# Third norm from undivided rows, and a reordered end of the convolution tiles

## The reference, cut to what matters

```python
h_res = h_res + (silu(gu[..., :D_FF]) * gu[..., D_FF:]) @ w_down   # "down"
x = rmsnorm(h_res, final_norm_w)                                   # end of block 1
h = rmsnorm_2(x, norm_even)                                        # the third norm is both of these
a_val, a_glu, a_gate, b_val, b_gate = split(h @ w_in_even)
u = a_val * sigmoid(a_glu)                                         # "glu": eight pairs of units
u = causal_depthwise_conv(u, conv_w, conv_b)                       # 31 taps
```

## Time and profile before

| What | us |
|---|---|
| median of three runs | 1782.23 (1780.98 to 1783.13) |
| the profiled execution | 1781.74 |
| its span, first to last instruction | 1779.70 |
| PE busy | 1726.0 (97%) |
| DVE busy | 830.3 (47%) |
| ACT busy | 679.4 (38%) |
| POOL busy | 862.9 (48%) |

### The profile page before, as it was taken

One profiled execution on the slowest core, in us unless ns is written; L12 is line 12 of the kernel. 1 busy time (PEld: TensorE's weight loads), 2 busy tenths in 40 slices (PEclk: granted clock), 3 DMA queues, 4 the chain that ended last, 5 costly groups with the idle time before them and its releaser, 6 DMA issues.

```text
span 1779.7 us, 22744 instructions
## 1 busy us (share of the span) xinstructions
PE 1726.0 (97%) x9103; PEld 1453.8 (82%) x9103; DVE 830.3 (47%) x1329; ACT 679.4 (38%) x997; POOL 862.9 (48%) x482
## 2 busy tenths in 40 slices
PE   7999899999999999999999999999999999999997
PEld 7888789889988888877888887877887778888886
DVE  7678955724333201112111112116999963357753
ACT  5656443232232222234222223223233444356651
POOL 3456443232334544544555555445459566356661
PEclk9999989999999999999999999998999999999999
DMA  5475377444322224222222223331222322222332
GB/s 198 140 233 167 88 227 231 117 150 148 114 66 84 94 92 141 91 92 95 95 94 94 93 92 101 96 106 62 94 94 94 108 86 92 95 96 95 96 100 76
DMA packets 120720, 201.39 MB, mean 113 GB/s; under 512 B 32512, under 2 KB 71576, under 8 KB 120616
## 3 DMA queue, kind: packets, MB, share of 16 engines
q1 hardware_dynamic: 119128, 197.47, 35.1%
q10 hardware_dynamic: 1488, 2.48, 0.4%
HBM read 170.46 MB, written 29.46 MB: 112 GB/s over the span
## 4 chain that ended last, share of the span: by engine, by line
PE 87%; DVE 7%; ACT 2%; issue 1%; DMA 1%; SPq 1%; POOL 0%; DVEq 0%; ACTq 0%; POOLq 0%
PE ps L403 72%; PE ps L1741 4%; DVE cacc L2170 2%; PE ps L877 1%; DVE inv L617 1%; DMA d_p<-dec 1%; DVE prd L614 1%; PE ps L930 1%; PE ps L923 1%; PE ps L909 1%; PE ps L887 1%; PE ps L917 1%; PE ps L934 1%; PE ps L895 1%; PE ps L885 1%
## 5 line engine op out<-in xcount | busy, mean ns | idle before, releaser
L391 POOL TENSOR_TENSOR w_lo<-w_raw,w_hi 128x1024 fp32r<-128x1024 f32 x264 | 634.4, 2411 | 537.1 <-ACT w_hi L385 536.9
L403 PE MATMUL ps<-hp_hi,w_hi 128*128 128x512 f32 (+2 forms) x1664 | 557.5, 363 | 2.1 <-DVE cacc L2170 1.5
L403 PE MATMUL ps<-hp_lo,w_hi 128*128 128x512 f32 (+2 forms) x1664 | 552.6, 360 | 0.0
L403 PE MATMUL ps<-hp_hi,w_lo 128*128 128x512 f32 (+2 forms) x1664 | 552.4, 359 | 0.0
L403 PEld LDWEIGHTS ps<-hp_hi,w_hi 128*128 128x128 f32 x1664 | 297.0, 190 | 57.2 <-issue 6.1
L403 PEld LDWEIGHTS ps<-hp_lo,w_hi 128*128 128x128 f32 x1664 | 296.8, 190 | 50.6 <-issue 1.7
L385 ACT ACTIVATE w_hi<-w_raw 128x1024 fp32r<-128x1024 f32 x264 | 277.6, 1054 | 157.0 <-DMA w_raw<-in_w 148.2
L403 PEld LDWEIGHTS ps<-hp_hi,w_lo 128*128 128x128 f32 x1664 | 296.6, 190 | 48.2
L1223 DVE SCALAR_TENSOR_TENSOR ps<-u_in,par,ps 128x511 f32<-128x511 f32 (+14 forms) x240 | 176.6, 739 | 8.4 <-ACT ps L1215 0.9
L2170 DVE SCALAR_TENSOR_TENSOR cacc<-ps,par,cacc 128x528 f32<-128x528 f32 x96 | 73.6, 766 | 34.5 <-ACT cacc L1789 31.8
L2552 POOL TENSOR_TENSOR y_lo<-tmp,y_hi 128x512 fp32r<-128x512 f32 x22 | 28.4, 1292 | 105.5 <-ACT y_hi L1953 105.5
(11 more groups left out here) (403 smaller groups left out, 2542.6 us busy)
## 6 DMA issues: line engine op xcount, KB each, us to landing
w_raw<-in_w SPq DMA_DIRECT2D x264, 512.0 KB, 3.5
d_y<-zero SPq DMA_DIRECT2D x6, 688.0 KB, 6.1
d_x<-zero SPq DMA_DIRECT2D x6, 688.0 KB, 5.9
d_at<-at SPq DMA_DIRECT2D x16, 256.0 KB, 2.9
d_kc<-kc SPq DMA_DIRECT2D x16, 256.0 KB, 3.1
d_qd<-eg SPq DMA_DIRECT2D x16, 256.0 KB, 3.1
d_p<-dec SPq DMA_DIRECT2D x16, 256.0 KB, 3.2
AT<-d_at SPq DMA_DIRECT2D x16, 256.0 KB, 5.7
```

The costliest lines, as they stand in the source:

```text
L391: e.tensor_tensor(w_lo[:, u % RAW, :], w_raw[:, u % RAW, :], w_hi[:, u % RAW, :].bitcast(F32), ALU.subtract).then_inc(s_lo, 1)
L403: mm = e.matmul(ov, w, r[:, k, t0:t1], start=(first and n == 0 and p3 == 0), stop=(last and n == len(tiles) - 1 and p3 == 2))
```

## The change

**The end of the tiles.** For tiles 15 to 22 ACT rounds the unit of tile n+2 behind `act_tap(n)` and no longer at the start of its iteration. In iteration 23 ACT first does `act_tap(23)`, the rounding, `act_vtm(2)` and `act_msb(0)`, and only then the silu of tile 22. `act_pg(4)` moves from behind the tiles to iteration 24, in front of `act_vt(3)`; `pe_pk(4)` moves from between `pe_msa(1)` and `pe_yx(0, 0)` to between `pe_vt(3)` and `pe_vtm(3)`.

**The third norm.** While `down` runs, ACT rounds x times the two weights, undivided, to h_hi, and DVE subtracts h_lo. PE begins `glu` with these; the column sums stand behind its first unit and the spread behind its second. The products of the first three pairs are multiplied in PSUM by the token's factor, row(7), on DVE (`pair_scaled`). Beside that DVE divides the eight rows into yb, ACT rounds n_hi, POOL subtracts n_lo, and pairs 3 to 7 and all later units up to `bgate` multiply these. The convolution steps are dealt out as 4, 10, 10 and five times 13 in `glu`, and 35 in place of 20 behind `bval`. Several buffers change their address; in the second mixer n_hi and n_lo take the place of h_hi and h_lo.

```diff
+GLU_STEPS = [4, 10, 10, 13, 13, 13, 13, 13]
 BV_STEPS = [4, 4, 3, 15, 7, 10, 14, 28]
 BG_STEPS = [6, 6, 6, 6, 5, 2, 0, 0]
...
-        24: [("pgp", 4), ("vt", 3), ("vtm", 3)]}
+        24: [("pgp", 4), ("pgq", 4), ("vt", 3), ("pkp", 4), ("vtm", 3)]}
...
+        h0 = top[0]
         hp_hi = put("hp_hi", [P, KT, T1 + 4], F32R)
         hp_lo = put("hp_lo", [P, KT, T1 + 4], F32R)
...
-        mx_lo = z("mx_lo", [P, 2 * KT, SEQ], 3 * K16, F32R)
+        mx_lo = at("mx_lo", [P, 2 * KT, SEQ], h0, F32R)
         u_in = z("u_in", [P, KT, SEQ], K16)
-        sg_a = z("sg_a", [P, KT, SEQ], 3 * K16)
+        sg_a = at("sg_a", [P, KT, SEQ], h0)
+        n_hi = z("n_hi", [P, KT, SEQ], 3 * K16, F32R)
+        n_lo = z("n_lo", [P, KT, SEQ], 4 * K16, F32R)
         yb = z("yb", [P, KT, SEQ], 5 * K16)
         pv = z("pv", [P, KT, 16 + SEQ], 5 * K16)
...
@@ -1517,7 +1521,6 @@
 
             pe_t(e, 0, 0, 32)
             pe_msa(e, 1)
-            pe_pk(e, 4)
             pe_yx(e, 0, 0)
             pe_msb(e, 1)
...
-            e.wait_ge(*ad.at("down", 2 * KT - 2))
-            pe_cols(e, row(7), 0).then_inc(ss.sem, 1)
-            pe_cols(e, row(4), 4).then_inc(ss.sem, 1)
-            e.wait_ge(*rc.at("n3", 5))
-            pe_spread(e, 5, 32).then_inc(tb_.sem, 1)
-
-            e.wait_ge(*dv.at("down", KT))
...
             u = BASE["glu"]
-            e.wait_ge(s_lo, u + 2)
-            for lo_part in (False, True):
-                for k in range(KT):
...
+            for j in range(KT):
+                rows, width = ((h_hi, h_lo), TOK) if j < 3 else ((n_hi, n_lo), ALL)
+                ready = {0: lambda k: hh.at("n3u", k + 1), 3: lambda k: lo.at("n3", k + 1)}.get(j)
+                e.wait_ge(*(dv.at("glu", j - 1) if j >= 2 else dv.at("down", 2 * j + 5)))
+                gemm(e, u + 2 * j, [ps[:, 2 * (j % 2), :]], width, *rows, K8, ready=ready).then_inc(s_pe, 1)
+                if j == 0:
+                    e.wait_ge(*ad.at("down", 2 * KT - 2))
+                    pe_cols(e, row(7), 0).then_inc(ss.sem, 1)
+                    pe_cols(e, row(4), 4).then_inc(ss.sem, 1)
+                e.wait_ge(*(ev.at("glu", j - 1) if j >= 2 else dv.at("down", 2 * j + 6)))
+                gemm(e, u + 2 * j + 1, [ps[:, 2 * (j % 2) + 1, :]], width, *rows, K8).then_inc(s_pe, 1)
+                if j == 0:
+                    e.wait_ge(*rc.at("n3", 5))
+                    pe_spread(e, 5, 32).then_inc(tb_.sem, 1)
 
             for j in range(KT):
                 e.wait_ge(*(ev.at("bval", j - 3) if j >= 4 else ev.at("glu", 7 + j // 2) if j % 2 else dv.at("glu", 7 + j // 2)))
-                gemm(e, BASE["bval"] + j, [ps[:, j % 4, :]], TOK, h_hi, h_lo, K8).then_inc(s_pe, 1)
+                gemm(e, BASE["bval"] + j, [ps[:, j % 4, :]], ALL, n_hi, n_lo, K8).then_inc(s_pe, 1)
...
-                if n < len(TILES):
+                if n < 15:
                     round_unit(e, n + 2)
+                if n == 23:
+                    act_tap(n)
+                    round_unit(e, n + 2)
+                    act_vtm(e, 2)
+                    act_msb(e, 0)
...
-                    if n != 3:
+                    if n not in (3, 23):
                         act_tap(n)
+                    if 15 <= n < 23:
+                        round_unit(e, n + 2)
...
-                    if task == "vtm":
+                    if task == "vtm" and n != 23:
...
-                    if task == "msb":
-                        act_msb(e, arg)
-                    if task == "pg":
+                    if task in ("pg", "pgq"):
                         act_pg(e, arg)
...
-            act_pg(e, 4)
             act_tc(e, 0, 0, 32)
...
+                if j == 0:
+                    e.wait_ge(*dg.at("g2", 1))
+                e.activation(h_hi[:, j, META:T1], x[:, j, :], ACT.Copy, scale=small[:, 36 + j:37 + j]).then_inc(hi.sem, 1)
...
+            round_unit(e, BASE["glu"] + 2)
+            round_unit(e, BASE["glu"] + 3)
             e.wait_ge(*ss.at("n3", 2))
             e.activation(small[:, 16:20], ps[:, 4, 4:8], ACT.Sqrt, bias=eps_col).then_inc(rt.sem, 1)
             e.wait_ge(*rc.at("n3", 3))
             e.activation(small[:, 28:32], small[:, 24:28], ACT.Sqrt, bias=eps_col).then_inc(rt.sem, 1)
-            for k in range(KT):
+            round_unit(e, BASE["glu"] + 4)
+            e.wait_ge(*tb_.at("n3", 1))
+            e.activation(row(7), ps[:, 5, :], ACT.Copy).then_inc(rt.sem, 1)
+
+            def divided_hi(k):
                 e.wait_ge(*hh.at("n3", k + 1))
-                e.activation(h_hi[:, k, META:T1], row(k), ACT.Copy).then_inc(hi.sem, 1)
+                e.activation(n_hi[:, k, :], yb[:, k, :], ACT.Copy).then_inc(hi.sem, 1)
+
...
-                round_unit(e, BASE["glu"] + 2 * j + 2)
-                round_unit(e, BASE["glu"] + 2 * j + 3)
-                e.wait_ge(s_pe, BASE["glu"] + 2 * j + 2)
+                if j >= 2:
+                    round_unit(e, BASE["glu"] + 2 * j + 2)
+                    round_unit(e, BASE["glu"] + 2 * j + 3)
+                e.wait_ge(*(fd.at("n3", 2 * j + 1) if j < 3 else (s_pe, BASE["glu"] + 2 * j + 2)))
                 if j >= 2:
...
-                if j in (3, 5):
-                    act_uc(e, (j - 3) // 2)
-                    act_c0(e, (j + 1) // 2)
+                if j == 0:
+                    for k in range(KT):
+                        divided_hi(k)
+                        if k == 3:
+                            round_unit(e, BASE["glu"] + 5)
+                if j in (4, 7):
+                    act_uc(e, (j - 4) // 3)
+                    act_c0(e, 2 + (j - 4) // 3)
 
...
+                if j >= 1:
+                    e.wait_ge(*hi.at("n3u", j))
+                    e.scalar_tensor_tensor(h_lo[:, j - 1, META:T1], x[:, j - 1, :], small[:, 35 + j:36 + j], h_hi[:, j - 1, META:T1].bitcast(F32),
+                                           ALU.mult, ALU.subtract).then_inc(hh.sem, 1)
...
-            e.wait_ge(*dg.at("g2", 1))
-            e.wait_ge(*tb_.at("n3", 1))
-            for k in range(KT):
-                e.scalar_tensor_tensor(row(k), x[:, k, :], small[:, 36 + k:37 + k], ps[:, 5, :], ALU.mult, ALU.mult).then_inc(hh.sem, 1)
-
+
+            def pair_scaled(j, part):
+                b = 2 * (j % 2) + part
+                e.wait_ge(s_pe, BASE["glu"] + 2 * j + 1 + part)
+                e.tensor_tensor(ps[:, b, :], ps[:, b, :], row(7), ALU.mult).then_inc(fd.sem, 1)
+
+            def divided(k):
+                e.scalar_tensor_tensor(yb[:, k, :], x[:, k, :], small[:, 36 + k:37 + k], ps[:, 5, :], ALU.mult, ALU.mult).then_inc(hh.sem, 1)
+
+            e.wait_ge(*rt.at("n3", 3))
             n0 = 0
             for j in range(KT):
+                if j < 3:
+                    pair_scaled(j, 1)
+                    if j == 0:
+                        divided(0)
+                    pair_scaled(j, 0)
+                    e.wait_ge(*fd.at("n3", 2 * j + 2))
                 e.wait_ge(*ev.at("glu", j + 1))
                 e.tensor_tensor(u_in[:, j, :], row(j % 2), ps[:, 2 * (j % 2), :], ALU.mult).then_inc(dv.sem, 1)
-                conv_steps(e, n0, 13)
-                n0 += 13
+                if j == 0:
+                    for k in range(1, KT):
+                        divided(k)
+                conv_steps(e, n0, GLU_STEPS[j])
+                n0 += GLU_STEPS[j]
 
             e.wait_ge(*dv.at("glu", KT))
             for r in range(4):
@@ -2386,8 +2415,8 @@
                 n += 1
                 conv_steps(e, n0, BV_STEPS[j])
                 n0 += BV_STEPS[j]
-            conv_steps(e, n0, 20)
-            n0 += 20
+            conv_steps(e, n0, 35)
...
-            for k in range(KT):
+            def divided_lo(k):
                 e.wait_ge(*hi.at("n3", k + 1))
-                e.tensor_tensor(h_lo[:, k, META:T1], row(k), h_hi[:, k, META:T1].bitcast(F32), ALU.subtract).then_inc(lo.sem, 1)
+                e.tensor_tensor(n_lo[:, k, :], yb[:, k, :], n_hi[:, k, :].bitcast(F32), ALU.subtract).then_inc(lo.sem, 1)
+
             for j in range(2 * KT):
                 split_unit(e, BASE["glu"] + j + 2)
+                if j in (2, 3):
+                    for k in range(4 * (j - 2), 4 * (j - 2) + 4):
+                        divided_lo(k)
```

More of the change, by code:

```diff
@@ L1675, in pe_program @@
                 e.wait_ge(*(dv.at("bgate", j - 3) if j >= 4 else ev.at("pool", j + 5)))
-                gemm(e, BASE["bgate"] + j, [ps[:, j % 4, :]], TOK, h_hi, h_lo, K8).then_inc(s_pe, 1)
+                gemm(e, BASE["bgate"] + j, [ps[:, j % 4, :]], ALL, n_hi, n_lo, K8).then_inc(s_pe, 1)
                 if j in (0, 4, 7):
@@ L1706, in pe_program @@
                         e.wait_ge(*l_sg.at(3 * g - 2 + i))
-                    gemm(e, BASE[f"xr{g}"] + i, [ps[:, xr_bank(g, i), :]], TOK, h_hi, h_lo, K8,
+                    gemm(e, BASE[f"xr{g}"] + i, [ps[:, xr_bank(g, i), :]], ALL, n_hi, n_lo, K8,
                          ready=(lambda k: hh.at("n4", k + 1)) if g == 0 and i == 0 else None).then_inc(s_pe, 1)
```

(6 more changed lines are left out.)

48 lines of the change are left out of this document (16 added, 32 removed).

## The result

The changed kernel takes 1771.09 us, the median of six runs (1767.55 to 1774.78), where the kernel before, beside it, takes 1783.15: a ratio of 0.9931, 95% interval 0.9917 to 0.9945. That is 12.1 us faster; forecast were 13.0, and 1769.0 with a range of 1762.0 to 1775.5. The profiled execution took 1772.52 with a span of 1770.7 (before 1779.7), so the two profiles show only 9 of the 12 us. The lines of the code have moved on: L407 is the product of a weight unit (L403 before), L395 POOL's split (L391), L1227 a step of the convolution (L1223), L1231 act_uc (L1227).

The account below looks back on a forecast made before the run. PE, busy 97% of the span, bounds the kernel, so edits pay only where it waits. Tail 5.8 plus third norm 7.2 (11.79 - 1.1 - 3.45) gives 13.0 us: 1769.0, range 1766.0 to 1771.5 (wider 1762.0 to 1775.5).

Parts of the forecast that it names:

- Third norm on PE: From the end of `down` to `glu`'s first pair: 25.46 us becomes 13.67, gain 11.79, part of it clock.
- The blocked add: Third norm: POOL's split holds up DVE's last `row(7)` add, so PE waits 1.1 us before the column sums (0 to 2.4).
- DVE up to `glu`: After the third norm's spread: the convolution starts 8 us later, about 1219, and nothing is late in `glu`.
- The debt of 15 steps: Convolution steps moved behind `bval`: ACT waits for DVE, PE waits 2.85 before `pool` 2 and 0.6 more; cost 3.45 us (0 to 8).
- Two covers: Behind `bval`: lateness of act_uc(4) in `agate` hidden by 0.6 us, that of `bgate` 4's wait hidden by 0.35.
- (a): QKV tail: moving pe_pk(4) off the chain between pe_msa(1) and pe_yx gains 3.72 us (1.9 to 5.4).
- (b): QKV tail: act_tap(23) no longer queues behind tile 22's silu, DVE's 1.30 us wait goes; counted only as cover for (a).
- (c): Tiles 15 to 22: rounding behind act_tap keeps splits off the substitution, which ends 2.1 us earlier (-2.4 to +4.3).
- The tail: End of the QKV tiles and first slots: 3.72 from (a) plus 2.1 from (c), 5.8 us gained and carried through the slots.
- The sum: Whole kernel: 5.8 plus 7.2 us is 13.0 faster; profiled 1781.74 becomes 1768.7, stated as 1769.0.
- the clock falls in the wait at `pool`: Rival: PE's clock drops in the new 2.85 us wait at `pool`, price 3.7 us, giving 1772.4; chance 0.10.
- The locks undo (a) and (c): Rival, QKV tail: DVE and POOL blocking each other leaves the tail's gain at 0, giving 1774.5; chance 0.08.

Follow-up runs that it names:

- deal: Changed kernel with convolution steps dealt out otherwise (more in `glu`, `bgate`'s first product ahead of steps) and ACT's copies 4 and 5 later; 1768.89 us.
- uc45_late: Changed kernel with act_uc(5), act_c0(7) moved behind `pool` 1's evictions and act_uc(4), act_c0(6) to `agate` 4; end of `down` to span's end 580.3 us for 576.8.
- r17_back: Changed kernel with only unit 17's rounding (tile 15's turn) back in front of the silu; ratio 0.9914 to the kernel before.
- r17_pk_back: r17_back with pe_pk(4) and its exponentials also back between pe_msa(1) and pe_yx; ratio 0.9938 to the kernel before.
- round_back: Changed kernel with the roundings of tiles 15 to 22 back in front of the silu and the tap; ratio 0.9950 to the kernel before.
- the second trace: The changed kernel as it is, profiled and timed again beside later variants; median 1768.18 us.

## Why the prediction was right, step by step

- **Third norm on PE, 11.79.** Measured 25.46 - 13.87 = 11.59. Right, its part through the clock too (13.7 us at 1.2 GHz around the old norm, none around the new one).
- **The blocked add, 1.1.** Did not occur: PE has no gap there in any of the twelve traces of the new third norm. The split starts at 1197.51 as placed, but DVE's instructions stand back to back there, and POOL's took 3.04 instead of 2.40: the split was held up, not the add.
- **DVE up to `glu`.** The convolution starts at 1215.61, 7.87 behind the spread (8 forecast), and nothing was late in `glu`: DVE stood idle for 1.38 and 2.11 before pairs 2 and 3.
- **The debt of 15 steps, 3.45.** The wait at `pool` was 3.11 for 2.85, with the cause as named (deal and uc45_late show it). Two covers were thinner than I said. act_uc(4), hidden by 0.6, cost 0.7: not through the rounding, but through sg_a, whose eviction stands behind it. In all the stretch grew by 236.5 - 231.4 = 5.1. Of that 3.1 and 0.7 are the waits named, 0.4 one that the trace puts down to issue. Most of the other 0.9 lies at the same three places: a matmul's row is 0.16 longer than the 0.233 from start to start, so each idle time is 0.16 short, and the first matmul behind it takes some 0.1 more (1389.55 to 1389.88, and not 0.233). The term is mis-sized by 1.6, the add of 1.1 did not occur: 11.59 - 5.1 = 6.5 against 7.2 (E-D: 6.6).
- **(a) pe_pk(4), 3.72.** 4.8 in the comparison of r17_back and r17_pk_back, one trace each, inside its bounds (1.9 to 5.4) and near the upper one, for the reason given there: L881 and L824 get the clock back.
- **(b)** The wait of 1.30 before the taps of tile 23 is gone and the taps of 22 and 23 run back to back (214.31 to 220.55). It was more than cover: by round_back, its rounding of unit 25 behind the tap frees one step and ends the substitution 2.2 earlier. The prediction saw this block go, but took it for replaced by one of unit 24 and gave (b) nothing.
- **(c) The roundings, 2.1.** This step failed. One blocked step of 2.42 is left of four, the one forecast for unit 24; the block forecast at tile 17 did not come. Tile 15's taps came late as forecast (1.47 for 1.7). Yet the substitution ends only 0.8 earlier, measured from A (54.5 for 55.2), and by round_back the moved roundings of (c) alone make it 1.4 later. What I did not follow was PE: I let DVE be even again by tile 19 and took the tiles for DVE's. Tile 17 waits for those taps, and after a gap of 2.95 runs in part at 1.2 GHz. It costs 3.0 and PE's tiles end 0.5 later than before, not earlier. Of the 0.7 that the scatter still gained, the weight load took the rest. X came no earlier, so (b) and (c) together were worth 0. With unit 17 left alone they are worth 2.7 (B-A 63.37), with the load moved 3.6.
- **The tail, 5.8.** 5.05 in the second trace (C-A), 0.2 in the first, where slot 0 at the low clock took 4.4 of it. That the sum came out near the second trace is luck: (a) was larger by 1.1 and (c) smaller by 2.1.
- **The sum.** 1768.7 and 0.5 make 1769.2 and not 1769.0, which changes nothing.
- **Rivals.** That the clock falls in the wait at `pool` happened in four of the nine traces that have this wait; by E-D it cost nothing in two of them (576.8) and 1.1 to 1.2 in two (577.9 and 578.0), less than the 3.7 of the rival. "The locks undo (a) and (c)" came for (c) alone, and there through the two small instructions and PE, not through the substitution's steps.

Where are the 3 us between 9 and 12? Each run has its span and mean granted clock. One line through the spans of 115 runs of all kernels, with a level for each kernel, falls by 1.34 us for each 0.001 of clock and leaves a standard deviation of 1.0 us, of 3.2 without it. At a clock of 0.988 the kernel before stands at 1777.5 and the changed one at 1770.6 to 1770.9, some 6.8 apart; the other 5 to 6 go with the clock, on the mean 0.985 before and 0.989 to 0.990 after. The low clock of the old third norm (13.7 us at 1.2 GHz in both of its traces, none there with the new one) can be the larger part of that. So the 13.0 of the forecast, summed from rows of one trace, was met in part by luck: it agrees with 12.1 for medians that hold this difference of clock. What else makes before's unprofiled runs slower than its profiled one (0.986) stays open: there is one trace of it.

## What to carry to other kernels

Behind each moved instruction follow not only who waits for it but the next gap of PE: here one that grew from 1.5 to 3 us cost its growth and as much again in clock. A debt of steps on an engine with little room does not go away when the first instruction that waits for it is moved; pay it where that engine idles, and put first what others wait for. And before a theory is made of one trace, take a second one of the same kernel: here the two differ by 4.9 us up to the last wait of slot 0, more than most of the edits.
